# A fused two-block transformer kernel: raw row turns with the norm factor on the sums, mixer steps shifted by a round, branch sums read tile by tile

## What is computed

```python
def rms_norm(x, g):
    y = xf * lax.rsqrt(jnp.mean(xf * xf, axis=-1, keepdims=True) + EPS)
    return (y * g.astype(jnp.float32)).astype(x.dtype)
...
def hybrid_layer(x, ...):
    hn = rms_norm(x, norm1_g)
    proj = hn @ w_in                      # 15 pieces, some 8200 columns
    ...
    log_a = jax.nn.log_sigmoid((g_a @ gla_a_up + gla_a_b)) / GLA_GATE_NORM
    y_gla = rms_norm(gla_mixer(...)) * silu(g_g)        # gated linear attention, chunks of 64
    y_moba = moba_mixer(rope(rms_norm(q)), rope(rms_norm(k)), v)   # causal softmax, 8 heads
    y_mlstm = rms_norm(mlstm_mixer(conv(q, k), v, log_i, log_f)) * sigmoid(l_o)
    gates = jax.nn.sigmoid(br_gate + gate_b)
    mixed = (gates[:, :, 0] * (y_gla @ w_br_gla) + gates[:, :, 1] * (y_moba @ w_br_moba)
             + gates[:, :, 2] * (y_mlstm @ w_br_mlstm))
    x = x + mixed @ w_out
    h2 = rms_norm(x, norm2_g)
    x = x + jnp.square(jax.nn.relu(h2 @ w_ff1)) @ w_ff2
    return x
```

## Time and profile before

| | us |
|---|---|
| median of 3 runs | 1737.35 (1737.33 to 1739.22) |
| the profiled execution | 1738.81 |
| its span in the trace | 1736.9 |
| PE busy in the span | 1564.4 (90%) |
| DVE busy | 1179.6 (68%) |
| ACT busy | 878.0 (51%) |
| POOL busy | 133.9 (8%) |

### The profile page before, as it was taken

How to read it: one execution, slowest core, us unless ns; L and a number is a source line. 1 busy time by engine, 2 the same in 40 slices (tenths; PEclk the granted TensorE clock), 3 DMA queues, 4 the chain that set the end, 5 groups by cost and what they waited for, 6 DMA issues and landing times.

```text
span 1736.9 us, 19887 instructions
## 1 busy us (share of the span) xinstructions
PE 1564.4 (90%) x7216; PEld 1257.6 (72%) x7216; DVE 1179.6 (68%) x1521; ACT 878.0 (51%) x1139; POOL 133.9 (8%) x133
## 2 busy tenths in 40 slices
PE   4998999989997898999989999777796999999995
PEld 4776777778886676777768887656685788777774
DVE  4676666767776678667757777556465655789995
ACT  4433556454444543466354444434633444677873
POOL 0442000000000055000000000000000000000000
PEclk9998999999998998999999999888997999999998
DMA  6442434456775243434366677513212555699991
GB/s 257 146 146 97 146 122 146 169 205 256 280 268 221 100 151 119 145 123 138 132 223 237 256 264 266 196 71 121 77 69 93 187 177 186 246 352 350 359 352 61
DMA packets 45440, 326.06 MB, mean 188 GB/s; under 512 B 5280, under 2 KB 5280, under 8 KB 6688
## 3 DMA queue, kind: packets, MB, share of 16 engines
q1 hardware_dynamic: 38304, 278.94, 44.7%
q0 software_dynamic: 4608, 33.56, 4.9%
q10 hardware_dynamic: 2432, 12.30, 1.8%
HBM read 323.73 MB, written 1.05 MB: 187 GB/s over the span
## 4 chain that ended last, share of the span: by engine, by line
PE 51%; issue 33%; DVE 9%; ACT 5%; DMA 1%; POOL 0%; POOLq 0%; DVEq 0%; ACTq 0%; SPq 0%
PE PS L147 48%; PE PS L152 4%; ACT S L161 2%; ACT w_hi L161 2%; DVE PR L168 1%; DVE qk L179 1%; DVE G L168 1%; DVE w_lo L168 1%; ACT L161 1%; DVE qk L173 1%; DVE S L179 0%; DVE PR L183 0%; DMA stage<-wall 0%; DVE S L168 0%; DVE X L168 0%
## 5 line engine op out<-in xcount | busy, mean ns | idle before, releaser
L168 DVE TENSOR_TENSOR w_lo<-stage,w_hi 128x1024 fp32r<-128x1024 f32 x532 | 653.3, 1233 | 387.7 <-ACT w_hi L161 379.4
L161 ACT ACTIVATE w_hi<-stage 128x1024 fp32r<-128x1024 f32 x532 | 560.9, 1059 | 565.9 <-PE PS L147 557.8
L147 PE MATMUL PS<-w_hi,a_hi 128*128 128x512 f32 x1088 | 446.3, 410 | 12.4 <-ACT PR L161 12.0
L147 PE MATMUL PS<-w_lo,a_hi 128*128 128x512 f32 x1088 | 429.8, 395 | 0.0
L147 PE MATMUL PS<-w_hi,a_lo 128*128 128x512 f32 x1088 | 429.5, 395 | 0.0
L147 PEld LDWEIGHTS PS<-w_hi,a_hi 128*128 128x128 f32 x1088 | 209.0, 192 | 63.1 <-ACT PR L161 13.7
L147 PEld LDWEIGHTS PS<-w_hi,a_lo 128*128 128x128 f32 x1088 | 207.6, 191 | 45.6
L147 PEld LDWEIGHTS PS<-w_lo,a_hi 128*128 128x128 f32 x1088 | 209.0, 192 | 41.1 <-issue 1.2
L147 PE MATMUL PS<-w_hi,h_hi 128*128 128x512 f32 (+1 forms) x480 | 193.8, 404 | 11.7 <-issue 6.0
L147 PE MATMUL PS<-w_lo,h_hi 128*128 128x512 f32 (+1 forms) x480 | 188.6, 393 | 0.0
L147 PE MATMUL PS<-w_hi,h_lo 128*128 128x512 f32 (+1 forms) x480 | 188.4, 393 | 0.0
(11 more groups left out here) (231 smaller groups left out, 1503.4 us busy)
## 6 DMA issues: line engine op xcount, KB each, us to landing
...
```

The lines of the kernel that those rows point to most:

```text
L147: ins = self.e.matmul(out, lhsT, rhs, start=start, stop=stop, skip_group_check=True)
L161: self.tell(self.e.activation(out, in_, func, **kw), sem, chain)
L168: self.tell(self.e.tensor_tensor(out, a, b, op), sem, chain)
```

## The change

1. **Norms of the first block.** norm_turn_* is replaced by raw_turn_*: PE turns X itself, in two parts of four 128-column blocks, and a_hi and a_lo carry the gain alone. The factor 1/rms of each row is put on the sums: as scale in ACT's evacuations and Relu, as a scalar in DVE's evacuations and gate sums, and, for the narrow product, by two small matmuls that spread it and a multiply. Squares, mean and power follow the turns. Before the feed-forward the first part of the turns stands ahead of the last half of mix_pe, and the first up product goes to HIGH instead of LOW.
2. **Mixer steps.** GLA's third exponential moves two rounds later, its outputs one round later; the mLSTM logs on DVE get a round of their own between the absolute value and the rest, and what follows in mLSTM moves a round later; the memset of the convolution's pad moves into the narrow step; moba starts beside the last GLA step, and each moba step stands about a round earlier; turn2 follows it at once; a wait for the branch turns moves from the start of softmax to its first turn.
3. **Sums.** branch_dve reads tile 0 on acc0 and signals for each tile; down_pe's last half computes columns 0 to 511 of both tiles first, and DVE adds in that order.

```diff
@@ -243,19 +243,20 @@
...
-    mlstm = [7] * 9 + [8] * 4 + [9] * 8
+    mlstm = [7] * 10 + [8] * 4 + [9] * 8
...
-    lanes = [[("gla", c) for c in gla] + [("moba", 5)] * 2 + [("turn0", 3)] + [("moba", 6)] * 13 + [("turn2", 6)],
-             [("rope", c) for c in rope],
-             [("mlstm", c) for c in mlstm] + [("turn1", 9)]]
+    lanes = [[(("gla",), c) for c in gla] + [(("gla", "moba"), 5), (("moba",), 5), (("turn0", "moba"), 6)] +
+             [(("moba",), 6)] * 12 + [(("turn2",), 6)],
+             [(("rope",), c) for c in rope],
+             [(("mlstm",), c) for c in mlstm] + [(("turn1",), 9)]]
...
-                order.append(lane.pop(0)[0])
-            if n != 1:
+                order += lane.pop(0)[0]
+            if n == 0 or n == 2 and lane:
@@ -574,6 +575,40 @@
...
+        def row_scale(t):
+            return st[:, 2 + t:3 + t]
...
+        def raw_turn_pe(p, n, i, ready):
...
+            for b in (2 * i, 2 * i + 1):
+                for j in range(2):
+                    for t in range(NT):
+                        k = 2 * b + j
+                        p.turn(PS[:, (SPARE + MID)[b], (2 * j + t) * P:(2 * j + t + 1) * P], X[:, t, k * P:(k + 1) * P], ident,
+                               sem="norm_turned" if (j, t) == (1, 1) else None)
...
+        def raw_turn_act(a, n, i, gain):
+            for b in (2 * i, 2 * i + 1):
+                a.wait_ge("norm_turned", 4 * n + b + 1)
+                for k in (2 * b, 2 * b + 1):
+                    a.act(a_hi[:, k, :], PS[:, (SPARE + MID)[b], (k % 2) * T:(k % 2 + 1) * T], scale=gain[:, k:k + 1],
+                          sem="norm_hi" if k % 2 else None)
...
+        def raw_turn_dve(v, n, i, gain):
+            for b in (2 * i, 2 * i + 1):
+                v.wait_ge("norm_hi", 4 * n + b + 1)
+                for k in (2 * b, 2 * b + 1):
+                    v.stt(a_lo[:, k, :], PS[:, (SPARE + MID)[b], (k % 2) * T:(k % 2 + 1) * T], gain[:, k:k + 1],
+                          r32(a_hi[:, k, :]), ALU.mult, ALU.subtract, sem="norm_lo" if k % 2 else None)
...
+        def mean_dve(v, n):
+            v.wait_ge("rows_squared", 2 * n + 2)
+            v.ts(st[:, 2:4], st[:, 0:2], 1.0 / D, EPS, ALU.mult, ALU.add, sem="rows_mean")
@@ -656,6 +691,11 @@
...
+            if use < DEPTH:
...
+                p.wait_ge("rows_rsqrt", norm + 1)
+                for t in range(NT):
+                    p.mm(PS[0:width, 7, tok(t)], row_scale(t).broadcast_to([P, width]), ident)
@@ -710,7 +750,8 @@
...
-                        a.act(chunk(CHUNKS[n])[:, 0, :], PS[:, turn_banks(n)[0], :], sem="evac0")
+                        a.wait_ge("rows_rsqrt", 2 * l + 1)
+                        a.act(chunk(CHUNKS[n])[:, 0, :], PS[:, turn_banks(n)[0], :], scale=row_scale(0), sem="evac0")
@@ -722,7 +763,8 @@
...
-                        v.copy(chunk(CHUNKS[n])[:, 1, :], PS[:, banks[1], :], sem="evac1")
+                        v.wait_ge("rows_rsqrt", 2 * l + 1)
+                        v.ts(chunk(CHUNKS[n])[:, 1, :], PS[:, banks[1], :], row_scale(1), None, ALU.mult, sem="evac1")
@@ -789,6 +831,7 @@
...
+            yield
@@ -810,20 +853,20 @@
...
             yield
+            yield
             a.wait_ge("gla_cum", l + 1)
             a.act(gdec.unsqueeze(2), g3[:, :, L - 1:L], ACT.Exp, scale=1.0 / 16)
-            a.act(gE3, gE3, ACT.Exp, scale=1.0 / 16)
             a.act(gE2, gE1, ACT.Exp, scale=-1.0 / 16)
...
             yield
-            yield
+            a.act(gE3, gE3, ACT.Exp, scale=1.0 / 16, sem="gla_exp")
             for _ in range(4):
...
             yield
-            for _ in range(6):
+            for _ in range(7):
                 yield
@@ -845,8 +888,8 @@
...
             yield
-            v.wait_ge("gla_exp", l + 1)
             for src in range(2):
+                v.wait_ge("gla_exp", 2 * l + src + 1)
                 for b in range(2):
@@ -1068,11 +1114,11 @@
...
                 yield
-
-            p.wait_ge("br_lo", 6 * l + 2)
+            p.wait_ge("moba_qk", 4 * l + 4)
+
             yield from softmax_pe(p, l, lambda h, t: TQ[half_rows(h), h // 2, tok(t)],
                                   lambda h, n: TK[half_rows(h), h // 2, 0:n],
-                                  lambda h, t: chunk(6)[:, t, h * HD:(h + 1) * HD], True, (1,))
+                                  lambda h, t: chunk(6)[:, t, h * HD:(h + 1) * HD], True, (1,), (("br_lo", 6 * l + 2),))
         def moba_act(a, l):
@@ -1200,7 +1247,6 @@
...
         def mlstm_dve(v, l):
-            v.fill(pad[:, :, 0:3], 0.0, sem="ml_set")
@@ -1330,24 +1377,29 @@
...
-                                 ((), ()) if half else [bank_free.get(b, ()) for b in banks[nh]])
+                                 ((), ()) if half else [bank_free.get(b, ()) for b in banks[nh]], tell0=half == 1)
...
-                        for b in banks[nh]:
-                            bank_free[b] = (("br_prod", prod + nh + 1),)
+                        for t, b in enumerate(banks[nh]):
+                            bank_free[b] = (("br_prod", 2 * (prod + nh) + t + 1),)
...
-        def branch_dve(v, b, first, acc, gate, gates_done, banks):
+        def branch_dve(v, b, first, acc, gate, gates_done, banks, sums):
...
-                v.wait_ge("used", v.half + 1)
...
-                    v.tt(acc[:, t, cols] if first else g, PS[:, banks[nh][t], :], g, ALU.mult, sem="br_prod" if t else None)
-                    if not first:
-                        v.tt(acc[:, t, cols], acc[:, t, cols], g, ALU.add, sem="br_sum" if t else None)
+                    if t == 0:
+                        v.wait_ge("acc0", sums + nh + 1)
+                    else:
+                        v.wait_ge("used", v.half + 1)
+                    v.tt(acc[:, t, cols] if first else gs[t], PS[:, banks[nh][t], :], gs[t], ALU.mult, sem="br_prod")
+                if not first:
+                    for t in range(NT):
+                        v.tt(acc[:, t, cols], acc[:, t, cols], gs[t], ALU.add, sem="br_sum" if t else None)
@@ -1382,15 +1435,21 @@
...
+                        if nh and kt == KD - 2:
+                            for go in last:
+                                go()
...
-            spent_act(a, 8)
...
+            spent_act(a, 7)
+            for go in last:
+                go()
+            spent_act(a)
@@ -1407,21 +1466,37 @@
...
+                    for go in last:
+                        go()
         def up_pe(p, norm, relu_base):
...
+                    if kt == 2:
+                        raw_turn_pe(p, norm, 1, (("x_sum", 4 * norm),))
...
-                project_half(p, LOW, kt, KD, free=((), ()) if kt else [(("ff_relu", relu_base - 1 + t),) for t in range(NT)],
+                project_half(p, LOW if norm is None else HIGH, kt, KD, free=((), ()) if kt else [(("ff_relu", relu_base - 1 + t),) for t in range(NT)],
...
         def down_pe(p, nk, first, final):
...
-                product(p, accs, h_hi, h_lo, k, [(0, W), (W, D)], first and k == 0, final and k == nk - 1, True)
+                if not (final and k == nk - 1):
+                    product(p, accs, h_hi, h_lo, k, [(0, W), (W, D)], first and k == 0, False, True)
+                    yield
+                    continue
+                slot = p.half % SPLITS
+                for n in range(2):
+                    wh, wl = (x[:, slot, n * W:(n + 1) * W] for x in (w_hi, w_lo))
+                    for t in range(NT):
+                        for i, (x, w) in enumerate(((h_hi, wh), (h_hi, wl), (h_lo, wh))):
+                            done = i == 2 and t == NT - 1
+                            p.mm(accs[t][n], x[:, k, tok(t)], w, False, i == 2, sem=("acc0", "used")[n] if done else None)
+                p.half += 1
@@ -1495,14 +1570,21 @@
             def hidden(i):
...
-                        a.wait_ge("acc0", sums0(l, 16 + i - FF_CHUNKS * l + 1))
+                        a.wait_ge("acc0", sums0(l, 22 + i - FF_CHUNKS * l + 1))
...
-                    a.act(relu[:, t, :], PS[:, 4 + t, :], ACT.Relu, sem="ff_relu")
...
-            spent_act(a, 3)
+                    a.wait_ge("rows_rsqrt", 2 * l + 2)
+                    a.act(relu[:, t, :], PS[:, (LOW if i % FF_CHUNKS else HIGH)[t], :], ACT.Relu, scale=row_scale(t), sem="ff_relu")
...
+            spent_act(a)
+            raw_turn_act(a, 2 * l + 1, 1, lay("g2"))
...
+            norm_act(a, 2 * l + 1, "x_sum", (8 * l + 3, 8 * l + 4), False)
+            spent_act(a, 2)
@@ -1524,7 +1606,10 @@
...
+            spent_dve(v)
+            raw_turn_dve(v, 2 * l + 1, 1, lay("g2"))
+            mean_dve(v, 2 * l + 1)
+            spent_dve(v, 2)
@@ -1542,9 +1627,12 @@
...
-            v.wait_ge("used", v.half)
-            for t in range(NT):
-                for n in range(2):
+            for n in range(2):
+                if n == 0:
+                    v.wait_ge("acc0", sums0(l + 1, 0))
+                else:
+                    v.wait_ge("used", v.half)
+                for t in range(NT):
@@ -1591,18 +1680,19 @@
...
```

(35 more changed lines are left out.)

54 lines of the change are left out of this document (30 added, 24 removed).

## The result

| | before | after |
|---|---|---|
| median, us | 1738.14 (1737.33 to 1739.22) | 1723.74 (1718.75 to 1723.87) |
| the profiled execution, us | 1738.81 | 1723.85 |
| its span | 1736.9 | 1722.0 |
| mean granted clock of its TensorE | 0.954 | 0.950 |

The ratio is 0.991, with a 95% interval of 0.9891 to 0.9929: faster by 0.9%, where 2.3% was forecast, and outside the range. So the forecast of 1697.3 was 20 to 26 us too fast.

The account below looks back on a forecast made before the run. The prediction took PE, busy 1564.4 of 1736.9 us, as the bound. Terms of 21.2 us for layer 0, 19.3 for layer 1 and -0.55 for block 2 total 40.0, giving 1697.3 us; range 1689 to 1702, chance 0.55.

Parts of the forecast that it names:

- GLA output a round later, gate logs split: GLA output: 12.8 us of state wait and low clock go, a 5.2 us spread wait comes; gain 4.9 a layer.
- Start of layer 0: Turns read X at once; matmuls start at 18.3, narrow product near 26.2 instead of 29.4; gain 2.8 us.
- Start of layer 1: Turns start after two sums, matmuls 4.75 us earlier; gain 3.6 us left at the narrow product.
- GLA exponentials: One exponential moves behind ACT's evacuation, still 1.4 us late; gain 3.0 us in layer 0, 0.6 in layer 1.
- Softmax: One round earlier, PE's two waits for a maximum, 2.5 us, go; net gain 0.9 and 0.6 us.
- Branch sums: Tile 0 is read early and signals alone, so six waits of 5.6 us go; gain 2.8 us a layer.
- Second norm: Before the feed-forward, hidden turn at 15.3 us instead of 21.6, with a 3.5 us wait; gain 4.6 a layer.
- Row factors: Row scaling costs nothing on DVE, 0.09 us per ACT operation, 18 a layer; loss 0.3 us a layer.
- DVE gives it back: From 100 to 136 us DVE is the limit, so PE's earlier arrival only waits later; 1705.9 us, chance 0.18.
- contention with POOL: DVE operations slow during POOL's RoPE; five more meetings of 1.7 us come to 8.6 us.
- The wait does not come back: At the mLSTM spread the 5.2 us wait and its low clock go, 7.25 a layer; 1682.8 us, chance 0.15.
- Slower: GLA's end and softmax's start share rounds; 26 softmax waits of 1.8 us give 1744 us, chance 0.03.

Follow-up runs that it names:

- e_after_again: The changed kernel run once more with no edit; 1717.81 us, ratio 0.9884.
- e_branch_only: The kernel before with only the branch sums as changed; 1729.00 us, ratio 0.9947.
- e_queue_order: Changed kernel with GLA's norm chain a round later, second-norm squares ahead of the lsm load, and first splits interleaved with a_hi and a_lo; 1692.69 us, ratio 0.9747.
- e_silu_free: The changed kernel with the Silu of GLA's gate taken in place, so ACT does not wait for DVE's norm chain; 1692.50 us, ratio 0.974.
- e_spread_later: e_queue_order with the mLSTM spread and its reading one round later, in the round of the column products; 1682.09 us, ratio 0.9677.

## Why the prediction was wrong, step by step

In one sentence: the step "GLA output a round later, gate logs split", priced as a gain of 4.9 us a layer, failed, because the same shift put ACT's Silu, which waits 4.07 and 5.36 us for DVE, ahead of two evacuations that PE needs; PE waited 1.83 and 3.25 us there in each layer, and the prediction has neither wait.

- **Start of layer 0: right.** The first matmul was forecast for 18.3 and the narrow product 2.8 us earlier; they came at 18.10, with DVE's a_lo as the last releaser, and 2.7 earlier.

```profile
18.10 0.77 PE L147 MATMUL PS<-w_hi,a_hi 128*128 128x512 f32 x1 [7.51 <-DVE a_lo L179]
```

- **Start of layer 1: right, a little small.** 4.4 for 3.6. PE waits 3.82 us for the second sum, the narrow product 0.90, which I had as 0.3 late.
- **GLA exponentials: the wait was right, the gain half of it.** Waits of 1.63 us in both layers where I had 1.4. But I had taken the low clock behind it as gone; it came at the evacuation before instead, where PE again waits 3.88. Gained 1.5 and -0.8 for 3.0 and 0.6; in e_after_again, with the same waits, 2.2 and -1.1, so up to a microsecond of each is the execution's clock.
- **Memset: right,** 2.7 a layer for 2.5.
- **GLA output and logs: the new wait was right in place and releaser, the step itself failed.** At the spread PE waits 3.50 us for ACT's last Exp, where I had 5.2, and 1.29 for a split where I had 0.6:

```profile
131.60 1.70 DVE L168 TENSOR_TENSOR w_lo<-stage,w_hi 128x1024 fp32r<-128x1024 f32 x1 [3.17 <-ACT w_hi L161]
...
133.40 0.47 PE L147 MATMUL PS<-w_hi,a_hi 128*128 128x512 f32 x1 [1.29 <-ACT w_hi L161]
...
145.77 1.20 PE L147 MATMUL PS<-iwa,csm 4*64 4x260 f32 x8 [3.50 <-ACT G L161]
```

The step that failed is "GLA output a round later": I followed it on PE only. The same shift moved GLA's norm chain on DVE, its power on POOL and its Silu on ACT. I had asked who waits for the outputs' state, not what is queued behind each moved instruction on its own engine. The prediction did note, under softmax, that the second Silu and moba's copies share a round on ACT, but priced that at 0.5 us and did not ask what the Silu waits for. Asked of ACT, the answer stood in the order of the program: the Silu, then evac0, with nothing or two short copies between. The size of ACT's wait could have been read before the run: ACT's idle time ahead of each Silu, 4.07 and 5.36 us, is in the trace of the kernel before too. I had given this term bounds of 0 and 12.8, "0, if it all returns". Against the 12.8 us that went stand, in layer 0, waits of 1.29, 3.50, 1.83 and 3.25 (9.9) and 10.2 us of work at half clock (5.1): the term came out some 2 us below zero. A bound below nothing was owed, since four engines' steps were moved.
- **Softmax: wrong, small.** I expected the waits to go (+0.9 and +0.6). In layer 0 1.44 us went, and 0.81 and 1.40 came, for DVE's gate sums (G<-PS,st,G), which now stand behind mLSTM's norm chain and a softmax step.
- **Branch sums: right, undersized.** 2.8 a layer from the waits; 4.1 and 4.2 in the two stretches by e_branch_only.
- **Second norm: right.** A wait of 2.89 us at the first hidden turn where I had 3.5, with the mean on DVE waiting for the squares as described:

```profile
347.75 1.06 ACT L161 ACTIVATE S<-X 128x1024 f32<-128x1024 f32 x1 [1.75 <-DVE a_lo L179]
...
350.18 0.17 DVE L175 TENSOR_SCALAR st<-st 128x2 f32<-128x2 f32 x1 [2.84 <-ACT S L161]
...
354.94 1.33 PE L152 MATMUL PS<-csm,PR 128*128 128x128 f32 x5 [2.89 <-DVE PR L168]
```

The gain was 5.1 and 5.3 for 4.6. ACT's wait for a_lo in front of the squares was in the sum (6.1 to 7.35, that is 1.25 us) and measures 1.75. It stands there only because the load of lsm needs it, which I overlooked; e_queue_order put the squares ahead of it.
- **Row factors: right on ACT for each operation, low in count, wrong on DVE.** A 128x512 evacuation or Relu on ACT takes 0.69 us on average with a per-partition scale, the evacuation 0.60 without. The figure of the Trainium skill that the prediction named, about 93 ns ("ScalarE: Activation LUTs", section "What ACT_TABLE_LOAD costs"), agrees with this difference of 0.09. The changed kernel has 26 such operations a layer, not 18. On DVE the factor was priced at nothing: the copy took 0.69 us, the scalar multiply in its place takes 0.75. What either costs PE is not shown.
- **Block 2: not settled.** -3.9 for -0.55 in this execution, and +1.7 in e_after_again, with the same program. The difference goes with the granted clock, 0.85 and 0.87 in that stretch.

Of the signs that the prediction named for being wrong, one came: PE waits 1.29 us for a split at 133.40, in the RoPE stretch. The sum itself had 0.6 us there, so this sign was set too sharp, and it did not point at the step that failed.

**The rivals.** "DVE gives it back" named the right stretch and the wrong reason: it was ACT's queue, and e_silu_free, in which DVE does the same operations in the same order, has no wait there. Its second form, contention with POOL, may show in the row above: the split took 1.70 us under POOL's RoPE, against 1.23 on average. The Trainium skill, "SBUF — State Buffer", section "SBUF: two separate sides", calls the shared port pair an exclusive lock; here it could explain at most 0.5 us of a wait of 1.29, and no run takes POOL away to show it. "The wait does not come back", 1682.8, was wrong for this kernel, whose spread did wait; e_spread_later shows that one more round takes that wait away. That its time, 1682.09, lies so near is chance, since it has three more edits. "Slower" looked at softmax rounds; steps that share a round did collide, but in two rounds a layer and not in 13, and by ACT's wait for GLA's norm chain.

Taken as a whole, the sum lacked one term. With it removed, e_silu_free ran at 1692.5, 5 us under the forecast of 1697.3. The mixer stretches then agree with the sum (8.2 and 7.7 for 8.6 and 8.3). That the total comes out lower is not the sum's merit: the second norms gained 6.6 and 6.8 for 4.6, with no low clock behind their waits, and block 2 gained 2.5 for -0.55.
